# Eight taps, a moved mean product, an unspread plan, an earlier window sum and two rerouted transfers in a two-block model

## The chip, the cores and the metric

The kernel runs on one core of a Trainium2 chip. The metric is the device time of one execution in microseconds (us), median of three runs. The engines are PE (matrix products), DVE (vector), ACT (scalar), POOL (GpSimd) and SP, which here only issues transfers.

## What is computed

Two blocks of two layers each, width 1024, 512 tokens (the second block has 256 context tokens more, 768 in all), all in float32. The parts that the change touches:

```python
def _multiscale_pool(z, pool_w, pool_scale):      # first block, layer 0
    pooled = jnp.stack([_centred_mean_minus_self(zf[:, :, g], w) for g, w in enumerate((2, 4, 8, 16))], axis=2)
    y = jnp.einsum('bsgc,gcd->bsgd', pooled, pool_w)
    return y.reshape(nb, s, B_WIDTH) * pool_scale

def _conformer_conv(h, w_in, dw, dw_b, ln_g, ln_b, w_out):   # first block, layer 1
    a, g = jnp.split(h @ w_in, 2, axis=-1)
    z = a * jax.nn.sigmoid(g)
    z = _depthwise_conv(z, dw, dw_b)               # 31 taps per channel
    z = jax.nn.silu(_layer_norm(z, ln_g, ln_b))
    return z @ w_out

# second block, each layer
h_lat = h_lat + ml[2] * rms_norm(o_lat, g_post_mix[i])
f_lat = sqrelu_mlp(modulate(h_lat, g_pre_ff[i], ml[3], ml[4]), w_ff1[i], w_ff2[i])
h_lat = h_lat + ml[5] * rms_norm(f_lat, g_post_ff[i])
```

## The kernel before

The program is a row of stages. Each is a block in which every engine has its own instruction list, ordered by semaphores, and a barrier of all engines ends it. The weight stream alone runs across barriers. SP loads 1 MB weight blocks into a ring of four (line 219), in the order of use, and waits before each load until the block that had the slot is used. ACT casts a piece of a block to a high part (lines 247, 248, 283), DVE subtracts to make the low part (lines 262, 263, 294, called the split here), and PE computes three products per pair. Two pieces are in flight, so ACT can cast a piece only when PE has used the piece before last, and PE needs DVE's split before it begins a piece.

Side work rides on the stream. The modulation matrices ("ada") come as side blocks between the weight blocks. DVE adds up a side block over the eight row groups in place (lines 315 and 317, eight steps for one vector, which sum_side splits in two halves of four), and PE finishes with four tiny products (line 429). When a host matrix is in SPREAD, the halves that wait are taken by turns, about one half after each piece. Otherwise all that wait are taken after the last piece of a block. PE's side products follow the piece at which the second half was taken, and they free the side block's slot in the ring. "up0" has 22 blocks of two pieces and hosts 24 side blocks. In the same stage DVE adds two of three taps of a short convolution (lines 1124, 1126) after ACT has written the centre tap (line 1103), and multiplies by the gelu on every second piece (line 1131).

The mixer of the first layer computes v by token, then z in four feature pieces, then the token mixing (line 1203), then u in four pieces. DVE normalises v (lines 1297 to 1299) between the splits. POOL makes the window sums of z (lines 1241, 1246, 1247), 18 instructions in four groups; the last operations of group g wait for product g-2 of PE (line 1208).

The conformer stage computes a gated z in eight channel tiles. The 31 taps of a tile are divided: the first PE_TAPS[j] are products with diagonal matrices on PE (line 1381; ACT makes the diagonals, line 1414), and DVE adds the others (lines 1436, 1438) to two running sums and joins them (line 1442). PE goes on to the column means by products with ones (line 1392). The next stage takes the mean (line 1483), subtracts it, squares on ACT, sums the squares on PE (line 1478), and so on.

In the second block the residual of 768 tokens (3 MB) is parked in device memory while its place is used for other data. It is brought back by a transfer: in the stage "out0" the 1 MB of the context, in "ff2_0" all 3 MB. Both are output stages: PE computes the product in two halves of 512 columns, and for the second half DVE works tile by tile (lines 1632 to 1637). Ahead of its first tile it waits for the transfer (`dve.wait_ge(brought, 16)`, line 1629). POOL issues the transfer after it has fetched the gate rows. In ff2_0 it first waits for the split that frees the borrowed place:

```python
def bring_back(pool, first, pieces, brought):
    pool.wait_ge(weights.lo_made, first + pieces // 2 + n_borrowed // 2)
    nc.gpsimd.dma_start(flat_of(resid), parked).then_inc(brought, 16)
```

`weights.load(sp, name)` issues all loads up to four blocks beyond the stage's own; the last of them waits for the stage's last split.

Of the kernel before, what the change touches and what calls it, by code (L numbers as in the profile page):

```python
# [23 lines left out]
ALU = mybir.AluOpType  # L24
# [7 lines left out]
D = 1024  # L32
DK = D // P
# [14 lines left out]
FFN = ((8 * D // 3 + 127) // 128) * 128  # L48
FK = FFN // P
CONV_W = 31  # L50
PE_TAPS = [8] * 6 + [11, 26]
DFF = 4 * D
HD = 64
GRID_W = 64
# [55 lines left out]
}  # L110


SPREAD = ["up0", "up1", "ab_v"]
THIRD_SLOT = ["ab_out", "down0", "cv_out"]


# [243 lines left out]
def build(nc, dram, out_dram, debug=None):  # L360
# [783 lines left out]
    def sgu_pool_mixer(hT, out_stage):  # L1144
# [4 lines left out]
        with stage():  # L1149
            mixT = sb("mixT", [P, DK, SEQ])  # L1150
            left = LeftOperand("ab_out", lambda k: mixT[:, k:k + 2, :], SEQ)
            with stage():
# [26 lines left out]
                with nc.Block() as block:  # L1179
# [46 lines left out]
                    @block.gpsimd  # L1226
                    def _(pool):
                        step = Chain(pool, pool_step)
                        nc.gpsimd.memset(z[:, :, 0:PAD], 0.0).then_inc(zeroed, 1)
                        nc.gpsimd.memset(z[:, :, PAD + SEQ:ZW], 0.0).then_inc(zeroed, 1)  # L1230
                        pool.wait_ge(loaded, 16 * n_loads)
                        pool.wait_ge(zeroed, 2)
                        pool.wait_ge(normed, LAT_T)
                        for g in range(4):
                            window = 2 << g
                            src = z[:, g, :]
                            pool.wait_ge(evac, Z0 + g + 1)
                            for level in range(g + 1):
                                lo, off = (2 << level) - 1, 1 << level
                                dst = sums[:, level % 2, :]  # L1240
                                step(nc.gpsimd.tensor_tensor(dst[:, lo:ZW], src[:, lo:ZW], src[:, lo - off:ZW - off], ALU.add))
                                src = dst
                            at = PAD + window // 2 - 1
                            if g >= 2:
                                pool.wait_ge(pool_mm, g - 1)
                            step(nc.gpsimd.tensor_tensor(pooled[:, g % 2, :], src[:, at:at + SEQ], inv_count[:, g, :], ALU.mult))
                            nc.gpsimd.tensor_tensor(pooled[:, g % 2, :], pooled[:, g % 2, :], z[:, g, PAD:PAD + SEQ], ALU.subtract).then_inc(pooled_made, 1)
                            pool.wait_ge(pooled_made, g + 1)
# [93 lines left out]

    def conformer_mixer(hT, affine, out_stage):
        HALF = CONV_W // 2
        MEAN_BANK = 0
        with stage():
            zc = sb("conv_out", [P, DK, SEQ])
            left = LeftOperand("cv_out", lambda k: zc[:, k:k + 2, :], SEQ)
            with stage():
# [10 lines left out]
                with nc.Block() as block:  # L1360
# [11 lines left out]
                    @block.tensor  # L1372
                    def _(pe):
                        def tap_products(j):

                            pe.wait_ge(diag_made, j + 1)
                            pe.wait_ge(evac, 2 * (j + 1))
                            if j >= 1:
                                pe.wait_ge(started, j)
                            for i in range(PE_TAPS[j]):  # L1380
                                last = nc.tensor.matmul(ps[SIDE_BANK][:], diag[:, j % 2, i, :], zp[:, j, i:i + SEQ],
                                                        start=(i == 0), stop=(i == PE_TAPS[j] - 1))
                            last.then_inc(taps_mm, 1)

                        def after_piece(piece):
                            if piece % 2 and piece > 1:
                                tap_products(piece // 2 - 1)
                        feature_products(pe, "cv_in", hT, [slice(0, SEQ)], evac, after_piece=after_piece)
                        tap_products(DK - 1)
                        for j in range(DK):  # L1390
                            pe.wait_ge(chained, j + 1)
                            nc.tensor.matmul(ps[MEAN_BANK][:], ones[:], zc[:, j, :], start=(j == 0), stop=(j == DK - 1))

                    @block.scalar
                    def _(act):
# [66 lines left out]
            with stage():  # L1462
                cols = sb("cv_ln_columns", [P, 2, DK])
                sq = sb("squares", [P, 2, SEQ])
                mean, inv = sb("mean", [P, SEQ]), sb("inv_std", [P, SEQ])
                loaded, centred, squared = sem("loaded"), sem("centred"), sem("squared")
                chained, var_ready, root_ready, normed, applied = sem("vector_step"), sem("var_ready"), sem("root_ready"), sem("normed"), sem("silu_done")
                sq_used = sem("square_used")
                with nc.Block() as block:
# [4 lines left out]
                    @block.tensor  # L1474
                    def _(pe):
                        for j in range(DK):
                            pe.wait_ge(squared, j + 1)
                            nc.tensor.matmul(ps[1][:], ones[:], sq[:, j % 2, :], start=(j == 0), stop=(j == DK - 1)).then_inc(sq_used, 1)

                    @block.vector  # L1480
                    def _(dve):
                        step = Chain(dve, chained)
                        step(nc.vector.tensor_scalar(mean[:], ps[MEAN_BANK][:], 1.0 / D, None, ALU.mult))
                        for j in range(DK):
                            nc.vector.tensor_tensor(zc[:, j, :], zc[:, j, :], mean[:], ALU.subtract).then_inc(centred, 1)
                        dve.wait_ge(sq_used, DK)
                        nc.vector.tensor_scalar(inv[:], ps[1][:], 1.0 / D, LN_EPS, ALU.mult, ALU.add).then_inc(var_ready, 1)
                        dve.wait_ge(root_ready, 1)
                        step(nc.vector.reciprocal(inv[:], inv[:]))
                        dve.wait_ge(centred, DK)  # L1490
                        for j in range(DK):
                            nc.vector.tensor_tensor(zc[:, j, :], zc[:, j, :], inv[:], ALU.mult).then_inc(normed, 1)
                        weights.lo_early(dve, "cv_out", left.share(0))
# [39 lines left out]
    def out_product_rms_stage(name, left, tiles, gates, bring_back=None, store=False):  # L1533
# [4 lines left out]
        with stage():  # L1538
# [13 lines left out]
            with nc.Block() as block:  # L1552
                @block.gpsimd
                def _(pool):
                    gate_rows_by_dma(pool, gates, spilled, gate_landed)
                    if bring_back is not None:
                        bring_back(pool, first, pieces, brought)

                @block.sync
                def _(sp):  # L1560
                    weights.load(sp, name)
                    if store:
                        for i, t in enumerate(tiles):
                            sp.wait_ge(added, i + 1)
# [79 lines left out]
    def ffn2_stages(layer, tiles):  # L1644
# [4 lines left out]
        with stage():  # L1649
# [8 lines left out]
            with stage():  # L1658
# [8 lines left out]
                with stage():  # L1667
# [3 lines left out]
                    with nc.Block() as block:  # L1671
# [23 lines left out]
                        def _(dve):  # L1695
# [7 lines left out]
                            if left.ahead:  # L1703
                                weights.lo_early(dve, down, left.share(0))
                            side_sums(dve, up)
            def bring_back(pool, first, pieces, brought):
                pool.wait_ge(weights.lo_made, first + pieces // 2 + n_borrowed // 2)
                nc.gpsimd.dma_start(flat_of(resid), parked).then_inc(brought, 16)
            out_product_rms_stage(down, left, tiles, gates2(layer, FF_GATE, 2 if n_borrowed else 1),
                                  bring_back if n_borrowed else None, store=layer == DEPTH - 1)  # L1710

# [1326 lines left out]
    def second_block():  # L3038
        for layer in range(DEPTH):
            tiles = all_tiles if layer == 0 else lat_tiles  # L3040
            streams = 2 if layer == 0 else 1
            with stage():
                bring = None
                if layer == 0:
# [3 lines left out]
                    left = LeftOperand("out0", lambda k: mixT[:, k:k + 2, :], TOK, ahead=False)  # L3048
                    dump("rwkv", mixT[:, 0:4, :])

                    def bring(pool, first, pieces, brought):
                        nc.gpsimd.dma_start(flat_of(resid)[:, 0:CTX_T * D], parked[:, 0:CTX_T * D]).then_inc(brought, 16)
                else:
                    mixT, left = odd_mixer()
                    dump("odd", mixT[:])
# [216 lines left out]
```

## Time and profile before

| what | value |
|---|---|
| median of three runs | 3683.64 us (3683.22 to 3686.53) |
| the profiled execution | 3686.53 us, span 3684.6 us |
| mean granted PE clock | 0.941 |
| busy: PE, DVE, ACT, POOL | 3230.6, 2201.8, 1289.6, 139.9 us |
| weight and data traffic | 342.67 MB, mean 93 GB/s |

The span runs from the first to the last instruction of one profiled execution; all positions below are us from its start. The line numbers are those of the kernel before.

### The profile page before, as it was taken

The numbers are of one execution on the slowest core, as the hardware profiler recorded it, in microseconds if no ns is written. First come the engines' busy times: TensorE is split into PE (matmuls) and PEld (weight loads), VectorE is DVE, ScalarE is ACT, GpSimd is POOL, SyncE is SP. The second block draws the span as 40 slices with busy tenths as digits, with TensorE's granted clock in tenths as the row PEclk, the third lists the DMA queues.
The fourth block names the chain that finished last, engine by engine and source line by source line (L and its number), as shares of the span: only waits on it lengthen the run. The fifth ranks groups of instructions, "written<-read, shape, count | busy, mean of one in ns | idle before, by whom it ended". The sixth has DMA issues, their size and how long they took to land. (4 is left out here: it accounts for less than half of the span.)

```text
span 3684.6 us, 62774 instructions
## 1 busy us (share of the span) xinstructions
PE 3230.6 (88%) x26414; PEld 2617.1 (71%) x26414; DVE 2201.8 (60%) x3942; ACT 1289.6 (35%) x2191; POOL 139.9 (4%) x180
## 2 busy tenths in 40 slices
PE   6989998988999958976776777999998999879999
PEld 5767876646887757844765766887887777658787
DVE  7678866785786466766445445554334556663344
ACT  2333334334333332154324325222234225642243
POOL 0200001000000001000101100000000000000000
PEclk8989999998999979988988998999999999989999
DMA  7524462202335212310000022322221242022231
GB/s 291 166 105 182 183 182 88 69 12 78 135 137 138 99 48 105 125 53 30 5 32 12 5 72 82 113 103 98 75 92 58 103 138 70 1 97 92 82 96 69
DMA packets 64424, 342.67 MB, mean 93 GB/s; under 512 B 15120, under 2 KB 16656, under 8 KB 28432
## 3 DMA queue, kind: packets, MB, share of 16 engines
q1 hardware_dynamic: 61616, 326.82, 26.1%
q0 software_dynamic: 2528, 11.84, 0.9%
q8 instruction: 209, 3.42, 0.4%
q14 instruction: 71, 0.58, 0.1%
HBM read 327.84 MB, written 10.79 MB: 92 GB/s over the span
## 5 line engine op out<-in xcount | busy, mean ns | idle before, releaser
L263 DVE TENSOR_TENSOR weight_lo<-weight_ring,weight_hi 128x1024 fp32r<-128x1024 f32 x341 | 423.0, 1242 | 152.5 <-ACT weight_hi L248 147.6
L248 ACT CAST weight_hi<-weight_ring 128x1024 fp32r<-128x1024 f32 x341 | 355.9, 1044 | 177.4 <-PE banks L420 91.9
L418 PE MATMUL banks<-hT_hi.1,weight_hi 128*128 128x512 f32 x896 | 365.9, 408 | 24.8 <-PEq L381 22.7
L419 PE MATMUL banks<-hT_lo.1,weight_hi 128*128 128x512 f32 x896 | 358.8, 400 | 0.0
L420 PE MATMUL banks<-hT_hi.1,weight_lo 128*128 128x512 f32 x896 | 358.5, 400 | 0.0
L418 PEld LDWEIGHTS banks<-hT_hi.1,weight_hi 128*128 128x128 f32 x896 | 171.4, 191 | 68.2 <-issue 25.7
L419 PEld LDWEIGHTS banks<-hT_lo.1,weight_hi 128*128 128x128 f32 x896 | 171.3, 191 | 41.5 <-issue 1.9
L420 PEld LDWEIGHTS banks<-hT_hi.1,weight_lo 128*128 128x128 f32 x896 | 171.0, 191 | 41.9
L418 PE MATMUL banks<-hT_hi.3,weight_hi 128*128 128x512 f32 (+1 forms) x512 | 175.5, 343 | 7.9 <-PEq L381 7.9
L419 PE MATMUL banks<-hT_lo.3,weight_hi 128*128 128x512 f32 (+1 forms) x512 | 174.3, 341 | 0.0
L420 PE MATMUL banks<-hT_hi.3,weight_lo 128*128 128x512 f32 (+1 forms) x512 | 174.3, 340 | 0.0
L317 DVE SCALAR_TENSOR_TENSOR side_sum<-weight_ring,silu_c2.1,side_sum 128x256 f32<-128x256 f32 x336 | 160.3, 477 | 0.0
L317 DVE SCALAR_TENSOR_TENSOR weight_ring<-weight_ring,silu_c2.1 128x256 f32<-128x256 f32 x336 | 160.2, 477 | 0.0
L517 PE MATMUL banks<-weight_hi,left_hi.6 128*128 128x512 f32 x360 | 144.5, 401 | 8.3 <-DVE weight_lo L263 8.3
L520 PE MATMUL banks<-weight_lo,left_hi.6 128*128 128x512 f32 x360 | 142.5, 396 | 0.0
L519 PE MATMUL banks<-weight_hi,left_lo.6 128*128 128x512 f32 x360 | 141.9, 394 | 0.0
L317 DVE SCALAR_TENSOR_TENSOR weight_ring<-weight_ring,silu_c1.1 128x256 f32<-128x256 f32 x280 | 135.6, 484 | 10.5
L418 PE MATMUL banks<-hT_hi.2,weight_hi 128*128 128x256 f32 (+1 forms) x352 | 123.6, 351 | 17.1 <-PEq L381 17.1
L420 PE MATMUL banks<-hT_hi.2,weight_lo 128*128 128x256 f32 (+1 forms) x352 | 122.0, 347 | 0.0
L419 PE MATMUL banks<-hT_lo.2,weight_hi 128*128 128x256 f32 (+1 forms) x352 | 122.0, 346 | 0.0
L262 DVE TENSOR_TENSOR left_lo.6<-ff_hidden.1,left_hi.6 128x1536 fp32r<-128x1536 f32 x24 | 42.2, 1760 | 130.9 <-ACT weight_hi L248 130.9
L2666 ACT COPY residual.1<-banks 128x512 f32<-128x512 f32 x120 | 70.3, 586 | 140.6 <-PE banks L2824 139.4
(744 smaller groups left out, 7759.1 us busy)
## 6 DMA issues: line engine op xcount, KB each, us to landing
weight_ring<-ff SPq DMA_DIRECT2D x64, 1024.0 KB, 4.9
weight_ring<-ada SPq DMA_DIRECT2D x48, 1024.0 KB, 5.0
weight_ring<-up SPq DMA_DIRECT2D x44, 1024.0 KB, 6.9
weight_ring<-ada_ffn SPq DMA_DIRECT2D x24, 1024.0 KB, 5.0
weight_ring<-down SPq DMA_DIRECT2D x20, 1024.0 KB, 4.9
weight_ring<-ada_mix SPq DMA_DIRECT2D x16, 1024.0 KB, 4.9
first_blocks.1<-ada_mix SPq DMA_DIRECT2D x8, 1024.0 KB, 11.8
weight_ring<-cv_in SPq DMA_DIRECT2D x8, 1024.0 KB, 5.0
```

The lines of the kernel that those rows point to most:

```text
L248: self.nc.scalar.copy(hi, raw).then_inc(self.hi_made, 1)
L262: self.nc.vector.tensor_tensor(x[2], x[0], x[1].bitcast(F32), ALU.subtract)
L263: self.nc.vector.tensor_tensor(lo, raw, hi.bitcast(F32), ALU.subtract).then_inc(self.lo_made, 1)
L317: ins = self.nc.vector.scalar_tensor_tensor(out=to, in0=w[:, k, :], scalar=vec[:, k, v:v + 1], in1=to, op0=ALU.mult, op1=ALU.add)
L418: nc.tensor.matmul(out, w_hi, x_hi, start=first, stop=False)
L419: nc.tensor.matmul(out, w_hi, x_lo, start=False, stop=False)
L420: return nc.tensor.matmul(out, w_lo, x_hi, start=False, stop=last)
L517: one = nc.tensor.matmul(out, xh, hi[:, kk, :], start=(k == 0), stop=False)
L519: nc.tensor.matmul(out, xl, hi[:, kk, :], start=False, stop=False)
L520: last = nc.tensor.matmul(out, xh, lo[:, kk, :], start=False, stop=(k == k_tiles - 1))
L2666: nc.scalar.copy(XT_flat[c % 2], pair(c, X_AT, 4 * CH)).then_inc(xt_copied[c % 2], 1)
```

## The change

Five edits in one. The last channel tile's taps on PE go from 26 to 18, so DVE gets 13 instead of 5. "up0" leaves SPREAD. POOL's window sums no longer wait for the normalised v. The eight mean products move from the end of the conformer stage to the start of the next, and DVE waits for them there. The two transfers that bring the residual back are issued by SP, behind the stage's weight loads, instead of by POOL.

```diff
-PE_TAPS = [8] * 6 + [11, 26]
+PE_TAPS = [8] * 6 + [11, 18]
-SPREAD = ["up0", "up1", "ab_v"]
+SPREAD = ["up1", "ab_v"]
                         pool.wait_ge(zeroed, 2)
-                        pool.wait_ge(normed, LAT_T)
                         for g in range(4):
...
                         tap_products(DK - 1)
-                        for j in range(DK):
-                            pe.wait_ge(chained, j + 1)
-                            nc.tensor.matmul(ps[MEAN_BANK][:], ones[:], zc[:, j, :], start=(j == 0), stop=(j == DK - 1))
...
                     @block.tensor
                     def _(pe):
                         for j in range(DK):
+                            last = nc.tensor.matmul(ps[0][:], ones[:], zc[:, j, :], start=(j == 0), stop=(j == DK - 1))
+                        last.then_inc(mm_mean, 1)
+                        for j in range(DK):
                             pe.wait_ge(squared, j + 1)
...
-                        step(nc.vector.tensor_scalar(mean[:], ps[MEAN_BANK][:], 1.0 / D, None, ALU.mult))
+                        dve.wait_ge(mm_mean, 1)
+                        step(nc.vector.tensor_scalar(mean[:], ps[0][:], 1.0 / D, None, ALU.mult))
...
                     gate_rows_by_dma(pool, gates, spilled, gate_landed)
-                    if bring_back is not None:
-                        bring_back(pool, first, pieces, brought)
 
                 @block.sync
                 def _(sp):
                     weights.load(sp, name)
+                    if bring_back is not None:
+                        bring_back(sp, first, pieces, brought)
...
-            def bring_back(pool, first, pieces, brought):
-                pool.wait_ge(weights.lo_made, first + pieces // 2 + n_borrowed // 2)
-                nc.gpsimd.dma_start(flat_of(resid), parked).then_inc(brought, 16)
+            def bring_back(sp, first, pieces, brought):
+                sp.wait_ge(weights.lo_made, first + pieces // 2 + n_borrowed // 2)
+                sp.dma_start(flat_of(resid), parked).then_inc(brought, 16)
...
-                    def bring(pool, first, pieces, brought):
-                        nc.gpsimd.dma_start(flat_of(resid)[:, 0:CTX_T * D], parked[:, 0:CTX_T * D]).then_inc(brought, 16)
+                    def bring(sp, first, pieces, brought):
+                        sp.dma_start(flat_of(resid)[:, 0:CTX_T * D], parked[:, 0:CTX_T * D]).then_inc(brought, 16)
```

## Rows read from the trace of the kernel before

**Rows 1.** Busy us, share of the span, instructions, of each engine.

```profile
PE 3230.6 (88%) x26414; PEld 2617.1 (71%) x26414; DVE 2201.8 (60%) x3942; ACT 1289.6 (35%) x2191; POOL 139.9 (4%) x180
```

**Rows 2.** Windows, the stretch of up0; PEclk is the granted clock.

```profile
core 0: us, PE busy (x) PEld busy (x) DVE busy (x) ACT busy (x) POOL busy (x), PEclk, DMA share, GB/s
...
210.00:490.00 280.00, 264.93 (x1161) 214.88 (x1162) 233.95 (x370) 95.97 (x123) 0.91 (x1) 0.96 0.48 176
```

**Rows 3.** Timeline of POOL in the mixer: start, duration, then idle and releaser.

```profile
104.96 1.84 POOL L1241 TENSOR_TENSOR window_sums.1<-z_padded.1 128x543 f32<-128x543 f32 x1 [60.11 <-DVE v.1 L1299]
...
122.05 1.09 POOL L1246 TENSOR_TENSOR pooled.1<-window_sums.1,inv_count.1 128x512 f32<-128x512 f32 x1 [2.02 <-PE banks L1208]
```

**Rows 4.** Timeline of ACT and DVE in the mixer.

```profile
89.53 0.58 ACT L1254 COPY z_padded.1<-banks 128x512 f32<-128x512 f32 x1
...
104.03 0.69 DVE L1299 TENSOR_TENSOR v.1<-v.1,sgu_bias.1 128x512 f32<-128x512 f32 x1
```

**Rows 5.** Timeline of POOL and DVE where both work, a later stage.

```profile
1461.25 1.59 POOL L2265 TENSOR_TENSOR qk_b.1<-qk_b.1,mixT.2 128x512 f32<-128x512 f32 x1 [0.63 <-DVE qk_b.1 L2309]
...
1450.62 1.36 DVE L315 TENSOR_SCALAR side_sum<-weight_ring,silu_c2.1 128x256 f32<-128x256 f32 x1
1452.02 0.35 DVE L315 TENSOR_SCALAR weight_ring<-weight_ring,silu_c2.1 128x256 f32<-128x256 f32 x1
...
1461.73 1.40 DVE L2326 SCALAR_TENSOR_TENSOR r.1<-gate_rows.1,recurrence_columns.1,r.1 128x255 f32<-128x255 f32 x1
```

**Rows 6.** Timeline of PE, the token mixing of the mixer.

```profile
106.00 3.82 PE L1203 MATMUL banks<-ws_transposed.1,v.1 128*128 128x128 f32 x32
```

**Rows 7.** Windows at up0's end and after the conformer: PEclk.

```profile
480.00:486.00 6.00, 0.00 (x0) 0.00 (x0) 5.27 (x9) 1.04 (x2) 0.00 (x0) 0.66 0.91 344
486.00:492.00 6.00, 5.84 (x14) 4.61 (x15) 2.42 (x3) 2.00 (x2) 0.91 (x1) 0.50 0.81 181
...
830.00:832.00 2.00, 1.68 (x4) 1.42 (x5) 0.06 (x1) 1.65 (x2) 0.95 (x1) 0.50 0.33 78
```

**Rows 8.** Timeline of DVE and ACT in up0: a normal, then the doubled block.

```profile
330.85 0.75 DVE L1124 SCALAR_TENSOR_TENSOR ffn_conv.1<-banks,ffn_taps.1,ffn_conv.1 128x511 f32<-128x511 f32 x1 [0.34 <-ACT ffn_conv.1 L1103]
...
332.30 1.22 DVE L263 TENSOR_TENSOR weight_lo<-weight_ring,weight_hi 128x1024 fp32r<-128x1024 f32 x1
...
336.10 0.78 ACT L1103 ACTIVATE ffn_conv.1<-banks,ffn_taps.1 128x512 f32<-128x512 f32 x1 [4.35 <-PE banks L420]
...
340.37 0.34 DVE L315 TENSOR_SCALAR weight_ring<-weight_ring,silu_c1.1 128x256 f32<-128x256 f32 x1
340.75 3.67 DVE L317 SCALAR_TENSOR_TENSOR weight_ring<-weight_ring,silu_c1.1 128x256 f32<-128x256 f32 x7
...
348.17 1.23 DVE L263 TENSOR_TENSOR weight_lo<-weight_ring,weight_hi 128x1024 fp32r<-128x1024 f32 x1 [2.31 <-ACT weight_hi L248]
```

**Rows 9.** Timeline of PE and DVE at the conformer's end.

```profile
797.42 7.03 PE L1392 MATMUL banks<-conv_out.1,ones.1 128*128 128x512 f32 x16
...
799.22 0.75 DVE L1438 SCALAR_TENSOR_TENSOR second_sum.1<-glu_padded.1,conv_taps.1,second_sum.1 128x512 f32<-128x512 f32 x1
...
800.55 0.75 DVE L1438 SCALAR_TENSOR_TENSOR second_sum.1<-glu_padded.1,conv_taps.1,second_sum.1 128x512 f32<-128x512 f32 x1
...
805.21 0.69 DVE L1483 TENSOR_SCALAR mean.1<-banks 128x512 f32<-128x512 f32 x1 [3.19 <-PEq L381]
```

**Rows 10.** Timeline of the queues of SP and POOL in out0 and ff2_0.

```profile
2239.82 0.33 SPq L219 DMA_DIRECT2D weight_ring<-ff  x1
...
2829.93 0.33 SPq L219 DMA_DIRECT2D weight_ring<-ada  x1
...
2729.40 0.53 POOL L1708 DMA_DIRECT2D residual.1<-parked_residual  x1 [150.63 <-DVE weight_lo L263]
```

**Rows 11.** DMA issues: count, KB each, median us from issue to landing.

```profile
weight_ring<-ada SPq DMA_DIRECT2D x48, 1024.0 KB, 5.0
...
parked_residual<-residual.1 SPq DMA_DIRECT2D x2, 3072.0 KB, 9.7
...
residual.1<-parked_residual POOLq DMA_DIRECT2D x1, 3072.0 KB, 12.0
```

**Rows 12.** Timeline of DVE, first tile of out0's and ff2_0's second half.

```profile
2242.39 0.16 DVE L1632 TENSOR_TENSOR inv_rms.1<-sums_of_squares.1 128x1 f32<-128x1 f32 x1 [1.40 <-ACT product.1 L1594]
...
2832.52 0.16 DVE L1632 TENSOR_TENSOR inv_rms.2<-sums_of_squares.2 128x1 f32<-128x1 f32 x1 [2.61 <-ACT product.2 L1594]
```

More of the change, by code:

```diff
@@ L1344, in conformer_mixer @@
         HALF = CONV_W // 2
-        MEAN_BANK = 0
         with stage():
@@ L1465, in conformer_mixer @@
                 mean, inv = sb("mean", [P, SEQ]), sb("inv_std", [P, SEQ])
-                loaded, centred, squared = sem("loaded"), sem("centred"), sem("squared")
+                loaded, mm_mean, centred, squared, mm_var = sem("loaded"), sem("mean_product"), sem("centred"), sem("squared"), sem("var_product")
                 chained, var_ready, root_ready, normed, applied = sem("vector_step"), sem("var_ready"), sem("root_ready"), sem("normed"), sem("silu_done")
```

## The prediction

> **What bounds the kernel now.** I read the totals first. PE is busy 88% of the span, DVE 60%, ACT 35%, POOL 4% [rows 1], so nearly everywhere the time is PE's, and an edit costs what it makes PE wait. Next came the stretch of "up0" among the windows: PE is busy for 265 of its 280 us and DVE for 234 [rows 2]. Last came the order of work inside each edited stretch (the timeline of one engine at a time), which shows how late the instruction that releases PE may be. Stages end in a barrier of all engines, and nothing runs across one but weight loads. A late stage therefore passes its whole delay on, and delays of different stages add.
>
> **Part 1: window sums freed from the norm.** POOL now begins at 104.96, right after DVE's last norm step (104.03 + 0.69 = 104.72) [rows 3, 4]. Without that wait it needs only the first z column, which ACT has copied by 90.1 (89.53 + 0.58) [rows 4]. Ten POOL instructions (3 for the first window, 4 for the second, 3 sums of the third) move from 105 to 120 us into 90 to 113 us. Everything behind them stays, because the multiply at 122.05 waits for PE's first pooled product [rows 3]; POOL's early finish buys PE nothing. The place they move to is where DVE is full: norm steps, splits and side sums nearly back to back until 104.72.
>
> What does DVE pay? A scalar_tensor_tensor of 255 elements, whose like comes every 0.51 us in a row of seven [rows 8], takes 1.40 us beside a POOL instruction that began at 1461.25 and ends at 1462.84; a tensor_scalar takes 1.36 us beside POOL and 0.35 us right after [rows 5]. The two exclude each other, instruction by instruction, at 0.9 to 1.0 us for each POOL instruction met. Nine of the ten meet DVE work (the first falls in DVE's wait for the root): 9 x 0.92 = 8.3 us later. The slack is small: the norm ends at 104.72 and PE's token mixing, which waits for it, starts at 106.00 [rows 4, 6]. So 8.3 - 1.3 = 7.0 us on PE. A split between the norm steps is late as well and stops PE earlier; that stall lies inside the 7.0. PE then idles some 5 us. At up0's end an idle PE was granted 0.66 of full speed and then 0.50 (the 1.2 GHz level) for 6 us of work [rows 7]; I add 1.0 for a part of that. **Part 1: +8** (bounds: five meetings and no clock loss, +3.3; ten at 1.01 and 2.5 for the clock, +11.3).
>
> The Trainium skill's page "SBUF — State Buffer" (Who interferes with whom) says that a DVE instruction contends with a GpSimd one that reads SBUF if it has two SBUF inputs or is in a two-port mode, and that the later one blocks fully. Read narrowly, by the first half alone, a norm step with one input would pass freely, and the term would lose some 1 us. The blocked tensor_scalar above has one SBUF tensor input, so the row bears out the second half, and I count all.
>
> **Part 2: up0 without the spread.** Each of 22 blocks (two pieces A, B) is followed by a side block, two of them by two: 24. A side block is 8 DVE steps (0.38 + 7 x 0.51 = 3.95 us). Now four follow the split of B and four that of the next A; afterwards all eight follow that of B. In a normal block the next A split, which ends at 333.52, is put off by 1.65 us to 335.17 (the eight end 2.0 later than the four, and DVE had 0.34 us of wait before 330.85) [rows 8]. PE wants it when B ends, about 335.9, as ACT reads B's bank at 336.10 [rows 8]. 0.6 us are left: no cost in about 20 blocks.
> At the doubled block 16 steps come in a row. From 340.37 they end at 348.3, two conv steps and the next split at 351.0. PE has finished B and its side products at 348.4, so it waits 2.6 us. Today it waits there too, some 1.6 us: the split comes at 348.17 because ACT's cast, and before it the weight load, is late [rows 8]. That load will start about 6 us sooner, since side blocks are freed one piece earlier. Net **+1** (bounds: -1.6, nothing left of today's wait; +8, 0.4 us in each of 20 blocks).
>
> **Part 3: the conformer's tail.** PE's last work today is 26 taps of 0.88 us each (two passes of 0.44), then 8 mean products of the same kind: 16 passes in 7.03 us, until 804.45; DVE takes the mean at 805.21, after the barrier (0.76), having been done 3.19 us before, at 802.02 [rows 9]. After the change PE does 18 taps and is free at 797.42 - 8 x 0.88 = 790.4. DVE's last convolution still starts where it did, behind the one before it, and has 13 taps instead of 5: 8 x 0.665 (half of 800.55 - 799.22 [rows 9]) = 5.3 us more, 802.02 + 5.3 = 807.3, barrier at 808.1. Of the 7.0 us taken off PE nothing arrives, for DVE has become the end of the stage. ACT's 8 fewer diagonals were hidden.
> Then the eight mean products, until now beside DVE's taps for all but 2.4 us, stand alone at the next stage's start: 16 passes, 7.0 us. PE comes to them after 17 us of idleness. After the 15 us one before 830.3 it was granted 0.50 from 830 to 832 [rows 7]. I take 3 us at half, 1.5 lost, and 0.3 for the first weight load. 808.1 + 7.0 + 1.5 + 0.3 = 816.9 against 805.21: **+12** (bounds: full clock +10; 6 us at half, as at up0's end, +13.5). By parts: 4 for the taps alone, 8 for the moved products.
>
> **Part 4: the residual brought back by SP.** The two transfers move from POOL's queue to behind SP's weight loads. Those run four blocks ahead, so the last one waits for the stage's last split: SP issues it at 2239.82 (out0) and 2829.93 (ff2_0) [rows 10]. Today POOL issues ff2_0's at 2729.40 [rows 10], 100 us ahead, and out0's right after the gate rows. Each ring wait of SP now holds the transfer too, and it then shares the DMA engines with the 1 MB load just ahead of it.
> In ff2_0: 3 MB plus 1 MB. The same 3 MB landed 12.0 us after POOL's issue, the 3 MB parked by SP 9.7 after its own, a lone load takes 5.0 [rows 11]. From 2830.3 I take 11.6, near POOL's: 2841.9. DVE waits for it before its first tile, which starts at 2832.52 today [rows 12]: +9.4 (bounds 9.7 and 14: +7.5 and +12). In out0: 1 MB plus 1 MB, 5.0 for one and 2.2 more for the second: 2239.8 + 7.2 = 2247.0 against 2242.39 [rows 12]: +4.6 (5.0 alone from 2240.2: +2.8; two of 5.0 in series: +7.4). DVE then works its six tiles one after another as before, ACT following it, and nothing later in the stage has slack. **Part 4: +14**. POOL's queue gains nothing; it carried nothing else that was waited for.
>
> The Trainium skill, same page (SBUF: two separate sides), says that POOL-issued transfers starve while DVE works in two-port mode and advises SP. If the 12.0 us contain such a wait, the transfer from SP lands sooner than I take, 9.7 giving +7.5; but it was issued 100 us ahead of its use, so there was no waiting to save.
>
> **The sum.** 8 + 1 + 12 + 14 = +35. The profiled execution took 3686.5 (span 3684.6), 2.9 above the median of 3683.64, so 3721.5 for its like and **3719** for a median.
>
> **Rivals.** (a) The shared port matters little: DVE meets four or five POOL instructions, part 1 is +3, total +30, 3714. For: the third window's sums may come when DVE is past its norm. Against: DVE is full there. (b) DVE becomes the bound of up0: each block's A split slips past PE's 0.6 us, 20 x 0.4 = 8 on top of 35: 3727. For: DVE is busy 234 of 280 us and gets 4 us bursts. Against: its waits stand behind the burst. (c) The clock: PE's new gaps leave it at half for 6 us in part 1, part 3 and once more after ff2_0, +6: 3725. (d) Not slower: the clock the other way. PE's mean grant is 0.94, up0's stretch has 0.96 [rows 2]; should the new gaps keep it at full level where it is now at half, 1 us returns for each 2 us of matmul, and 70 us of such stretches would be needed to meet 35; at 100 us it is 3669. For: nothing in the rows; up0 holds only some 20 of them. (e) Part 4 misses: the transfers land before DVE's last split, 14 less, 3705. Against: SP's queue cannot pass its load at 2829.93.
>
> **How the numbers follow.** Main case 0.60, (a) 0.13, (b) 0.09, (c) 0.10, (d) 0.02, (e) 0.06. The main case's own range adds neighbouring bounds, not all at one end: 3709 to 3729. Reaching to (a) to (c) and near (e): 3704 to 3732. About 0.2% (7 us) is what this measurement tells from no change; slower by more 0.96, within 0.02, faster 0.02.
>
> **What would show it.** Part 1: POOL's first sum near 91, DVE's 0.69 us steps at 1.3 to 1.6, mixing near 113. Part 2: eight sum steps in a row without a PE wait, one wait of 2 to 3 us. Part 3: DVE's final add at 807 on this scale, the mean products in the next stage, the first at half clock, 12 us from old to new mean. Part 4: DVE waits for a DMA at both places, 4 to 5 and 9 to 10 us. Wrong would be: no lengthened DVE steps, or a residual transfer that has landed when DVE asks.

## The result: 1.2% slower, and the profile after

The changed kernel took 3727.22 us (median of 4 executions, 3724.63 to 3731.65) and the kernel before, beside it on the same chip, 3684.35 (3683.22 to 3686.53): +42.9 us, ratio 1.0119, 95% interval 1.0106 to 1.0132. The forecast was 3719 with a range of 3704 to 3732. The profiled execution took 3725.03, with a span of 3722.9 against 3684.6 (+38.3) and a mean granted clock of 0.937 against 0.941. Positions below are us from the span's start; behind line 1232 the changed kernel's line numbers are one to five lower than those of the kernel before.

First the totals, from the page:

```profile
PE 3230.0 (87%) x26398; PEld 2617.4 (70%) x26398; DVE 2212.8 (59%) x3950; ACT 1287.0 (35%) x2183; POOL 138.8 (4%) x178
```

PE is as busy as in [rows 1], in a span 38 us longer: it waits more. To see where, take from PE's timeline the first product of each stage that follows a barrier:

```profile
145.34 0.47 PE L517 MATMUL banks<-weight_hi,left_ahead_hi.1 128*128 128x512 f32 x1 [1.52 <-PEq L381]
224.73 0.76 PE L418 MATMUL banks<-hT_hi.1,weight_hi 128*128 128x512 f32 x1 [7.94 <-PEq L381]
495.91 0.77 PE L517 MATMUL banks<-weight_hi,left_ahead_hi.2 128*128 128x512 f32 x1 [6.29 <-PEq L381]
640.16 0.77 PE L418 MATMUL banks<-hT_hi.1,weight_hi 128*128 128x512 f32 x1 [8.27 <-PEq L381]
854.26 0.76 PE L517 MATMUL banks<-weight_hi,left_ahead_hi.3 128*128 128x512 f32 x1 [15.27 <-PEq L381]
```

In the kernel before the same five products start at 137.23, 216.86, 486.16, 631.60 and 830.32. The lag grows to 8.1 over the mixer, to 9.8 over up0, falls to 8.6 over down0, and stands at 23.9 after the conformer. Then it stays at 24.1 to 24.5 as far as 1910, dips to 21.0 at 2156, in stages that no edit touches, and ends at 38.3 behind out0 and ff2_0. The loss lies in the edited places.

**The mixer.** Timelines of POOL, DVE and PE:

```profile
88.92 2.02 POOL L1240 TENSOR_TENSOR window_sums.1<-z_padded.1 128x543 f32<-128x543 f32 x1 [43.98 <-ACT z_padded.1 L1253]
91.01 1.37 POOL L1245 TENSOR_TENSOR pooled.1<-window_sums.1,inv_count.1 128x512 f32<-128x512 f32 x1
...
130.16 1.09 POOL L1245 TENSOR_TENSOR pooled.1<-window_sums.1,inv_count.1 128x512 f32<-128x512 f32 x1 [25.56 <-PE banks L1208]
```

```profile
90.50 0.72 DVE L1296 TENSOR_SCALAR v.1<-v.1,mean_var.1,inv_std.1 128x512 f32<-128x512 f32 x1
91.25 1.68 DVE L1297 TENSOR_TENSOR v.1<-v.1,sgu_gain.1 128x512 f32<-128x512 f32 x1
...
98.98 2.29 DVE L263 TENSOR_TENSOR weight_lo<-weight_ring,weight_hi 128x1024 fp32r<-128x1024 f32 x1
101.19 1.18 DVE L315 TENSOR_SCALAR weight_ring<-weight_ring,silu_c1.1 128x256 f32<-128x256 f32 x1
102.41 5.15 DVE L317 SCALAR_TENSOR_TENSOR weight_ring<-weight_ring,silu_c1.1 128x256 f32<-128x256 f32 x7
...
110.69 0.69 DVE L1298 TENSOR_TENSOR v.1<-v.1,sgu_bias.1 128x512 f32<-128x512 f32 x1
```

```profile
101.32 0.50 PE L418 MATMUL banks<-hT_hi.1,weight_hi 128*128 128x512 f32 x1 [2.52 <-DVE weight_lo L263]
...
111.52 6.40 PE L1203 MATMUL banks<-ws_transposed.1,v.1 128*128 128x128 f32 x32 [3.31 <-DVE v.1 L1298]
```

While POOL works (until 104.6), DVE's steps take 1.2 to 1.7 us (the first of them 0.72) and a split 2.29 instead of 1.22; behind the side sums they are back at 0.69 [rows 4]. PE now waits for DVE twice, and the token mixing takes 6.40 instead of 3.82 us [rows 6]. The windows show why: the granted clock, the third number from the end, was 0.50 over its first part, where the kernel before had 1.00.

```profile
111.00:114.00 3.00, 2.48 (x11) 2.51 (x12) 3.00 (x4) 0.00 (x0) 0.00 (x0) 0.50 0.47 194
```

At 130.16 POOL waits 25.6 us for PE: its head start bought nothing.

**Up0.** PE's only wait over 0.5 us between its first and last product:

```profile
358.51 0.50 PE L418 MATMUL banks<-hT_hi.1,weight_hi 128*128 128x512 f32 x1 [1.97 <-DVE weight_lo L263]
```

It stands behind 16 side steps in a row, the doubled block, where the kernel before waited 1.37 us. Behind the single blocks of eight steps PE does not wait. But the clock fell behind this wait, and it did not in the kernel before (1.00 from 349.5 to 352):

```profile
358.50:360.00 1.50, 1.49 (x5) 1.25 (x6) 1.37 (x2) 0.43 (x1) 0.00 (x0) 0.77 1.02 426
360.00:362.00 2.00, 2.00 (x6) 1.51 (x6) 1.99 (x3) 0.00 (x0) 0.00 (x0) 0.50 0.98 414
362.00:364.00 2.00, 2.00 (x9) 1.58 (x8) 1.79 (x5) 0.00 (x0) 0.00 (x0) 0.82 0.66 172
```

I estimate the loss from these rows at 1.5 x 0.23 + 2.0 x 0.50 + 2.0 x 0.18 = 1.7 us, more than the wait itself grew.

**The conformer's end.** DVE's last sum, PE's products, DVE's mean, and the granted clock over them:

```profile
816.05 0.69 DVE L1437 TENSOR_TENSOR conv_out.1<-conv_out.1,second_sum.1 128x512 f32<-128x512 f32 x1
827.64 0.69 DVE L1482 TENSOR_SCALAR mean.1<-banks 128x512 f32<-128x512 f32 x1 [10.90 <-PE banks L1472]
```

```profile
817.52 10.08 PE L1472 MATMUL banks<-conv_out.1,ones.1 128*128 128x512 f32 x16 [17.39 <-PEq L381]
829.78 9.21 PE L1476 MATMUL banks<-squares.1,ones.1 128*128 128x512 f32 x16 [2.17 <-ACT squares.1 L1500]
```

```profile
819.00:822.00 3.00, 3.00 (x5) 1.09 (x4) 0.00 (x0) 0.00 (x0) 0.00 (x0) 0.50 0.00 0
...
824.00:826.00 2.00, 2.00 (x6) 0.95 (x5) 0.00 (x0) 0.00 (x0) 0.00 (x0) 1.00 0.00 0
...
830.00:832.00 2.00, 2.00 (x4) 0.70 (x3) 2.00 (x5) 0.90 (x2) 0.00 (x0) 0.59 0.03 8
```

The mean products stand alone and take 10.08 us against 7.03 in [rows 9]. The clock was granted at 0.50, the 1.2 GHz level, until about 823, and near it again when the squares' products began after PE's next pause of 2.2 us; those took 9.21 us, 7.71 before. Whether that last loss belongs to the edit is taken up behind e5 and e6.

**Out0 and ff2_0.** SP's issues, and DVE's first tile:

```profile
2263.28 0.33 SPq L219 DMA_DIRECT2D weight_ring<-ff  x1
2263.66 0.43 SPq L3051 DMA_DIRECT2D residual.1<-parked_residual  x1
...
2857.89 0.33 SPq L219 DMA_DIRECT2D weight_ring<-ada  x1
2858.26 0.43 SPq L1707 DMA_DIRECT2D residual.1<-parked_residual  x1
```

```profile
2270.64 0.16 DVE L1631 TENSOR_TENSOR inv_rms.1<-sums_of_squares.1 128x1 f32<-128x1 f32 x1 [6.18 <-DMA residual.1<-parked_residual]
...
2870.65 0.16 DVE L1631 TENSOR_TENSOR inv_rms.2<-sums_of_squares.2 128x1 f32<-128x1 f32 x1 [12.78 <-DMA residual.1<-parked_residual]
```

The releaser is a DMA in both places. DVE idles 6.18 and 12.78 us where it idled 1.40 and 2.61 for ACT [rows 12]: 4.8 and 10.2 more.

### The profile page after: what moved, and what is told of

It reads as the page before. It is cut to its first block and busy times, and to the rows that moved or that the text cites. A ratio compares the mean times of both kernels' runs of the same rounds, so it can differ in the third digit from the quotient of the medians.

```text
span 3722.9 us, 62741 instructions
## 1 busy us (share of the span) xinstructions
PE 3230.0 (87%) x26398; PEld 2617.4 (70%) x26398; DVE 2212.8 (59%) x3950; ACT 1287.0 (35%) x2183; POOL 138.8 (4%) x178
```

## The experiments

Twelve kernels, each the kernel before with the edit named, in three groups of four; each group ran on a chip of its own with the kernel before beside it. That kernel's median was 3689.90 in the first group (21 executions, 3682.6 to 3694.2), 3687.60 in the second (27) and 3686.48 in the third (33, 3678.0 to 3694.9). Executions of one kernel thus spread by 12 to 17 us. I therefore give two numbers, the difference of the medians, and what the edited stage itself grew in the profiled execution, by the same stage starts as above. The second is the sharper one, but it is one execution each, and a stage that no edit touches can differ by 1 to 3 us between two profiles too.

### The parts one by one

**e1_pool**, window sums alone:

```diff
-                        pool.wait_ge(normed, LAT_T)
```

> The kernel before with the first edit alone: POOL's window sums no longer wait for the normalised v. Theory (POOL and DVE shut each other out, instruction by instruction, where DVE is full; then PE idles and restarts at half clock): +8 us over the kernel before, of which about 6.7 are DVE's delay of its last norm step and about 2.6 are the token mixing at the 1.2 GHz level (6.4 instead of 3.8 us), less the 1.3 of slack. Nothing after the mixer changes, so the whole run is +8. Rival (port matters little): +3. Rival (the delay is absorbed by the weight stream later, since the ring gets full while PE idles): under +4 in the whole run although the mixer is 8 longer.

Measured: 3699.99, +10.1 (ratio 1.0026, 1.0017 to 1.0035); the mixer +8.8. DVE's norm (first step to last) takes 20.9 us against 12.8; the mixing 6.45 us. As in the changed kernel. Both rivals are out: the lag is 11.1 us at 217 and 11.2 at 1574, so nothing is absorbed later. (Of these 11, 2.3 arose in the stage behind the mixer, which e2 and e3 show as well, without this edit.)

**e2_spread**:

```diff
-SPREAD = ["up0", "up1", "ab_v"]
+SPREAD = ["up1", "ab_v"]
```

> The kernel before with up0 taken out of SPREAD alone. Theory (eight side steps in a row cost nothing behind a normal block's split, and 1 us at the one doubled block): +1 to +2 us, from the stage of up0 alone, with perhaps some tenths given back in down0 (whose first loads came earlier), so the run is +0.5 to +2. Rival (DVE becomes the bound of up0, 0.4 us in each of 20 blocks): +8. Rival (the stage ends earlier since slots of the ring are freed earlier): -1.5.

Measured: 3691.25, +1.4 (1.0007, 0.9997 to 1.0016). Up0 +2.4, down0 -0.9, and the same wait of 1.97 us at the doubled block, with the same clock behind it: 0.80, 0.50 and 0.90 in 353.5 to 356, to 358 and to 360. DVE does not become up0's bound. The size of the first theory holds, but by terms that it did not have: the wait grew by 0.6 us, and the rest of the 2.4 is mainly this clock (1.7 us, estimated as above).

**e3_tail**: both conformer edits of the diff, nothing else.

> The kernel before with the conformer's edits alone: 18 taps instead of 26 for the last tile on PE, and the eight mean products moved to the next stage. Theory (DVE's 13 taps end the stage, then the mean products stand alone, at half clock since PE has idled 17 us, and the squares' products after them too): +14 to +15.5 us in this kernel as in the one with all edits, of which 4 are taps, 10 the mean products, 1.5 the squares' products. Rival (part of the 15 came from the other edits' disturbance, such as the clock or the ring's state): +12, as it was first estimated with only 3 us at half clock.

Measured: 3704.15, +14.3 (1.0034, 1.0021 to 1.0047); the stages from the conformer's start to cv_out's +14.0, with mean products of 9.49 us and squares' products of 9.37 us. The interval of the whole run, +8 to +17 us, holds the rival's +12 too; the stages speak for the theory, and the loss is the conformer's own.

**e4_sp**: the bring-back by SP, as in the diff.

> The kernel before with the bring-back by SP alone: the two transfers of the residual are issued by SP behind the stage's weight loads. Theory (they come late, since SP's queue holds them behind a load that waits for the stage's last split; DVE waits for the landing, and nothing after it has slack): +15 us, 5 in out0 and 10 in ff2_0. Rival (a wait of 5 and one of 10 are partly made good by weight loads that run ahead across the barrier): under +11.

Measured: 3704.28, +14.4 (1.0034, 1.0019 to 1.0048). DVE waits 6.26 and 12.44 us for the DMA. Nothing is made good later: the lag behind ff2_0, 16.7 us against the profile of before, is 16.8 at the end. The four parts alone add up to 10.1 + 1.35 + 14.25 + 14.4 = 40.1 of the 42.9 us: within the spread nothing points to an interaction.

### Where the bring-back stands in SP's queue

**e7_sp_early**: SP issues both transfers, but in out0 ahead of the stage's loads, and in ff2_0 amid them (`load` gets a limit `upto` for this, not shown):

```diff
+                    if bring_back is not None:
+                        middle = weights.pieces[first + pieces // 2 + 4][0] + RING + 1
+                        weights.load(sp, name, upto=middle if pieces > 16 else weights.loads)
+                        bring_back(sp, first, pieces, brought)
                     weights.load(sp, name)
```

> The residual brought back by SP as in the changed kernel, but not behind the stage's last weight load: in out0 ahead of the stage's loads, in ff2_0 amid them, as soon as the borrowed place is free (the load ahead of it waits for the same split). Theory (the cost of 15 us is the place in SP's queue, not that SP issues it): 0 within 2 us of the kernel before, DVE waits for no DMA at either place. Rival (SP's transfer of 3 MB stands ahead of weight loads in the same queue and delays them, so that PE waits in mid-stream): +2 to +10 in the stage of ff2_0. Rival (SP's transfers are slower in themselves): DVE waits in out0, +3.

Measured: 3686.54, -1.1 (1.0000, 0.9991 to 1.0010). SP issues at 2174.46 and 2745.95, and DVE waits for ACT again:

```profile
2241.90 0.16 DVE L1636 TENSOR_TENSOR inv_rms.1<-sums_of_squares.1 128x1 f32<-128x1 f32 x1 [1.41 <-ACT product.1 L1598]
...
2832.17 0.16 DVE L1636 TENSOR_TENSOR inv_rms.2<-sums_of_squares.2 128x1 f32<-128x1 f32 x1 [2.61 <-ACT product.2 L1598]
```

Between 2562 and 2840 PE is busy for 270.1 us, 269.7 in the kernel before, so the weight loads behind the 3 MB lose nothing either. The whole cost of part 4 is the place behind the last load, not the queue that issues.

### The conformer's tail taken apart

**e5_taps**:

```diff
-PE_TAPS = [8] * 6 + [11, 26]
+PE_TAPS = [8] * 6 + [11, 18]
```

> The kernel before with 18 instead of 26 taps for the last tile on PE, and nothing else; the mean products stay where they are and follow DVE's sums one by one. Theory (DVE's last convolution ends the stage, eight steps of 0.665 later; PE's last mean product waits for it): the mean is taken at 809 to 810 on the scale of the kernel before, +4 to +5, and PE, whose mean products wait for DVE, has idled enough for a part of them to run at half clock, which costs nothing as all but the last lie beside DVE. The run is +4 to +5. Rival (the half clock after PE's idle time is at its work here as well, 1.7 us or more on the last product and the squares' products): +6 to +7.

**e6_mean**: the mean products moved, 26 taps kept.

> The kernel before with the eight mean products moved to the next stage, and nothing else: PE keeps its 26 taps. PE is free at 797.4, DVE at 802.0, so PE idles 5.4 us instead of 17. Theory (the products cost 7.0 us alone and the half clock costs 3 more only after the long idle time): the mean at 802.8 + 7.0 + 0.3 = 810.1, +5, and after it no loss in the squares; the run +5. If the idle time of 5.4 us is enough for half clock: +8 at the mean, +9.5 in the run. Rival (taps and mean products add plainly, 4 and 11): +11.

Measured: e5 3696.93, +9.3 (1.0023, 1.0013 to 1.0033), its stages +8.0; e6 3695.83, +8.2 (1.0017, 1.0007 to 1.0026), its stages +6.1. Both miss. The taps alone cost about twice what was expected; the rival of e5 had the mechanism, but priced it at 6 to 7. These are the rows of PE's timeline in e5:

```profile
808.20 2.07 PE L1392 MATMUL banks<-conv_out.1,ones.1 128*128 128x512 f32 x2 [8.07 <-DVE conv_out.1 L1442]
813.17 9.98 PE L1478 MATMUL banks<-squares.1,ones.1 128*128 128x512 f32 x16 [2.90 <-ACT squares.1 L1501]
```

The last mean product alone comes after 8.07 us of waiting and takes 2.07 us, where the one before it took 1.12, and the squares' products 9.98 instead of 7.71; the clock stood at 0.50 from 808.2 to 816, through the pause between them. By stage starts, 5.8 of the 8.0 us had come by the mean and 2.3 came at the squares. In e6 the pause before the mean products was 5.20 us, and they took 8.67, between 7.03 and 10.08, while the squares' stayed at 7.71.

The squares' products need a caution. In seven of the nine profiles whose conformer is not edited (the kernel before, e1, e4, e7, e9, e10, e11) they took 7.70 or 7.71 us. In the other two, e2 and e12 below, they were slow behind the same pause:

```profile
812.33 9.40 PE L1478 MATMUL banks<-squares.1,ones.1 128*128 128x512 f32 x16 [2.89 <-ACT squares.1 L1501]
...
805.79 9.26 PE L1482 MATMUL banks<-squares.1,ones.1 128*128 128x512 f32 x16 [2.89 <-ACT squares.1 L1507]
```

So this half clock also comes without any edit to the conformer, in some executions. All four profiles with 18 taps on PE have it (9.21 to 9.98), which points to the taps, but how much of these 1.5 to 2.3 us is the edit's is not shown.

**e8_warm**: the tail of e3, and work for PE in the pause:

```diff
                         tap_products(DK - 1)
+                        pe.wait_ge(chained, 1)
+                        for _ in range(17):
+                            nc.tensor.matmul(ps[0][:], ones[:], zc[:, 0, :], start=True, stop=True)
```

> The conformer's edits as in the run of the tail alone (+14.3), and in PE's idle time of 17 us at the stage's end 17 products of 0.88 us into a bank that nobody reads (they add nothing to the output). Theory (3 us of the mean products and 1.5 of the squares are the half clock after that idle time): the granted clock stays at 1, the mean products take 7.0 instead of 10.1 us, the squares' phase 7.7 instead of 9.2, and the run is 4 to 4.5 below the tail alone, +10 over the kernel before. Rival (the 10.1 us are the products' own time when nothing runs beside them, reads of zc or the barrier): no change, +14.3.

Measured: 3700.82, +13.2 (1.0032, 1.0020 to 1.0044); the stages +13.0, 1.0 less than e3. The filler ran until 803.4, the barrier still made PE pause, and the clock fell behind that pause:

```profile
806.18 8.80 PE L1476 MATMUL banks<-conv_out.1,ones.1 128*128 128x512 f32 x16 [2.77 <-PEq L381]
817.15 9.21 PE L1480 MATMUL banks<-squares.1,ones.1 128*128 128x512 f32 x16 [2.17 <-ACT squares.1 L1504]
```

```profile
803.00:806.00 3.00, 0.40 (x1) 0.00 (x0) 2.36 (x4) 0.00 (x0) 0.00 (x0) 1.00 0.00 0
...
808.00:811.00 3.00, 3.00 (x5) 1.05 (x4) 0.00 (x0) 0.00 (x0) 0.00 (x0) 0.53 0.00 0
811.00:815.00 4.00, 3.98 (x10) 1.48 (x8) 0.00 (x0) 0.00 (x0) 0.00 (x0) 1.00 0.00 0
```

The rival (10 us is their own time) is refuted: at 0.53 three us hold five of the passes, at full clock four us hold ten. But the theory's size is refuted too: of 4.5 us the filler saved 1.0, and the squares' products gained almost nothing. At full clock behind the filler PE paused 2.77 us and the clock fell; it did not fall behind the 2.90 us ahead of the squares' products in the kernel before. The length of the pause alone does not decide.

### POOL's window sums by dose

**e9_three** and **e10_seven** put POOL's wait behind the first (`if g == 1`) and the second group (`if g == 2`), so 3 and 7 POOL instructions run beside the norm:

```diff
-                        pool.wait_ge(normed, LAT_T)
                         for g in range(4):
+                            if g == 1:
+                                pool.wait_ge(normed, LAT_T)
```

> The kernel before, with POOL's wait for the normalised v put behind the first of the four window groups: 3 POOL instructions instead of 10 run beside DVE's norm. Theory (each POOL instruction met costs DVE 0.9 to 1.0, and 1.28 us of slack lie before the token mixing): two or three met, 1.8 to 2.7 us later on DVE, so the mixing starts 0.5 to 1.4 later than before and at full clock; the mixer +0.5 to +1.5, the run within 0.2% of no change. Rival (an early POOL start costs as a whole, not by instructions met): +8 as with all ten.

> The same with POOL's wait behind the second group: 7 POOL instructions run beside DVE's norm. Theory: with all ten the norm's end came 6.7 later; seven of them give 4.5 to 6, of which 1.28 are slack, and the mixing starts 3.2 to 4.7 later; PE's wait before it is then 1 to 2.5 us, so it may keep the full clock. The mixer +3.5 to +7 (the upper end if the mixing runs at half clock). Rival (as a whole): +8.

**e11_warmmix**: all ten early, and a filler ahead of PE's wait for the norm:

```diff
+                        for _ in range(12):
+                            nc.tensor.matmul(ps[MIX0 % NROT][:, 0:P], ones[:], ones[:], start=True, stop=True)
                         pe.wait_ge(normed, LAT_T)
```

> The first edit alone (all ten POOL instructions early, +8.8 in the mixer's stage), and 12 products of ones by ones (128 columns) put ahead of PE's wait for the norm, into a bank that the token mixing then overwrites. They fill 3 us of PE's 3.3 us pause. Theory (2.6 us of the 8.0 are the token mixing at the 1.2 GHz level after PE's two pauses): the mixing takes 3.8 instead of 6.4 us and the stage is +5.5 to +6.2. Rival (the level falls by the pause of 2.5 us before it, which stays, or by what comes with the change on DVE): the mixing stays at 6.4 and the stage at +8.8.

PE's token mixing in e9, e10 and e11:

```profile
106.96 3.81 PE L1203 MATMUL banks<-ws_transposed.1,v.1 128*128 128x128 f32 x32 [0.69 <-DVE v.1 L1300]
```

```profile
109.86 6.65 PE L1203 MATMUL banks<-ws_transposed.1,v.1 128*128 128x128 f32 x32 [2.71 <-DVE v.1 L1300]
```

```profile
108.98 2.92 PE L1199 MATMUL banks<-ones.1 128*128 128x128 f32 x24
112.33 3.84 PE L1205 MATMUL banks<-ws_transposed.1,v.1 128*128 128x128 f32 x32 [0.42 <-DVE v.1 L1300]
```

| early POOL instructions | DVE's norm, us (before 12.8) | mixing, us | mixer | whole run |
|---|---|---|---|---|
| 3 (e9) | 14.8 | 3.81 | +0.9 | 3688.56, +2.1 (0.9993 to 1.0015) |
| 7 (e10) | 18.4 | 6.65 | +6.7 | 3692.07, +5.6 (1.0001 to 1.0019) |
| 10 (e1) | 20.9 | 6.45 | +8.8 | +10.1 |
| 10 and filler (e11) | 20.6 | 3.84 | +6.4 | 3694.22, +7.7 (1.0008 to 1.0028) |

The cost follows the dose: 2.0, 5.6 and 8.0 us of norm. The windows give the clock of the mixing: 0.50 from 110 to 113 in e10, 1.00 in e9 and e11. So the half clock is a cost of its own: filling PE's pause gives the mixing its 3.8 us back and takes 2.4 off the stage. Here 0.42 us lie between filler and work, and the filler did what it could not do in e8, where the barrier left 2.77.

### A version to beat both

**e12_keepwarm**: none of the edits, but fillers in pauses that the kernel before has: 13 products behind the squares' products, and at the end of each of the three stages that turn the normalised residual:

```diff
+                    pe.wait_ge(mod_act, HALF_F)
+                    pe.wait_ge(mod_dve, DK - HALF_F)
+                    for _ in range(3):
+                        nc.tensor.matmul(ps[2][:], ones[:], resid[:, tiles[0], 0:BANK], start=True, stop=True)
...
+                        for _ in range(13):
+                            nc.tensor.matmul(ps[2][:], ones[:], sq[:, 0, :], start=True, stop=True)
```

> The kernel before with none of the edits, and products that nobody reads in pauses of PE which it already has: 13 of 0.88 us in the 15.3 us behind the squares' products of the conformer, and 3 at the end of each of the three stages that turn the normalised residual (7.4 to 7.8 us of pause). The stages after these pauses begin at the 1.2 GHz level today and stay there for 3 to 6 us. Theory (the level follows what PE did just before, so work in the pause gives it back): 1 to 2 us less after the conformer and 1 to 3 us less at each of the three, -4 to -8 us, faster than both kernels. Rival (a pause of 2 to 3 us at the barrier is enough for the lower level, as in the run with the filled tail): 0 within 2 us.

Measured: 3686.51, +0.0 (0.9996, 0.9987 to 1.0005). The mean granted clock rose from 0.941 to 0.946, but not where it was wanted. Windows across the conformer's end:

```profile
814.00:826.00 12.00, 12.00 (x29) 5.16 (x28) 8.95 (x10) 7.16 (x9) 0.00 (x0) 1.00 0.00 0
826.00:830.00 4.00, 0.21 (x1) 0.00 (x0) 2.36 (x2) 3.57 (x6) 0.00 (x0) 0.93 0.00 0
830.00:836.00 6.00, 5.67 (x13) 4.46 (x14) 2.42 (x3) 1.99 (x2) 0.95 (x1) 0.50 0.71 177
```

Twelve us at full clock, a pause of 4 us at the barrier, and six us of real work at 0.50. The full clock was given to products that nobody reads. Behind the three stages with the other fillers the pauses were 3.98, 3.51 and 4.48 us, and the first 3 us of work were granted 0.74, 0.50 and 0.52, against 0.50 each before. This profile also has the slow squares' products (9.26 us). The rival holds. None of the kernels tried is shown to be faster than the kernel before.

## Why the prediction was right, and what it mis-sized

| | predicted | in the profiled execution | median of the part alone |
|---|---|---|---|
| 1, window sums | +8 | +8.1 | +10.1 |
| 2, up0 (with down0) | +1 | +1.9 - 1.2 = +0.7 | +1.4 |
| 3, conformer's tail | +12 | +15.4 | +14.3 |
| 4, bring-back | +14 | +4.8 + 10.2 = +15.0 | +14.4 |
| sum | +35 | 39.2, span +38.3 | 40.1, all together +42.9 |

**Part 1** came out at its number with its own terms a little off. DVE's norm stretched by 20.88 - 12.84 = 8.0 (forecast 8.3, nine meetings at 0.92), and the slack of 1.3 was there; but in the changed kernel's profile the norm also began 1.4 us sooner (90.50 against 91.88), so PE's mixing was 5.5 late instead of 7.0. The clock cost 2.6, not 1.0. These two misses cancel, and that is luck. In e1, where the norm began 0.8 sooner, the stage is +8.8. e9 to e11 show the mechanism and both terms. Rival (a), four or five meetings, is out: seven single steps are longer by 0.8 to 1.1 us each, and the seven side steps of line 317 by 1.5 together. The Trainium skill's page "SBUF — State Buffer" (Who interferes with whom) agrees in the reading that I took: a norm step with one SBUF tensor input, free by the narrow reading, took 1.46 us in e1 beside POOL and 0.55 otherwise. Who begins first matters as well: in e10 the same step began at 95.13, took 0.54 us, and POOL's sum of 95.26 took 1.35 instead of 1.09.

**Part 2** is right in its waits: none behind single blocks, one at the doubled block, 1.97 instead of 1.37, so 0.6 of the forecast 1.0. Its number is luck: the clock behind that wait, which it did not have, cost some 1.7 us more, and down0 came out 0.9 to 1.2 shorter in both profiles. I did not look for the cause of the latter; the profiles of e5 and e12, where up0 is not edited, have down0 1.4 us shorter too, so it need not come from the edit. Rival (b), +8 in up0, is out: e2's up0 grew by 2.4.

**Part 3** had the mechanism and the order of events: DVE's last sum ended at 816.74, 176.6 after the stage's start against 170.4 before, +6.2 (forecast 5.3, which e3 has); the barrier 0.8; then the products alone. Mis-sized is the step "I take 3 us at half, 1.5 lost". The products stood at half clock until about 823, some 6 us, and lost 3.0. The 0.3 for the first weight load did not show: the products began 0.8 after DVE's last sum, the barrier alone. To the mean that makes 13.9 instead of 11.7. And the prediction stopped at the mean, though the squares' products took 1.5 more, part of which may come without the edit (e2, e12). Rival (c), half clock for 6 us, came true in part 1 and here, but not behind ff2_0, where the first 3.3 us were at half before as well (0.50 then, 0.57 now); its 3725 is nearer to what was measured than the main case's 3719. The split "4 for the taps alone, 8 for the moved products" is wrong: alone they cost 8.0 and 6.1 (e5, e6). Each brings a pause and a half clock of its own; and that the taps' extra DVE time ends the stage was counted, but not that the last mean product then starts at half clock, and the squares' products perhaps by the same cause.

**Part 4** is right: issue behind the last load, landing 12.4 us after the issue (forecast 11.6), nothing later absorbs it, and e7 shows that the place in the queue is all of it. Rival (e) is out. The rule on transfers issued by POOL of the Trainium skill's page "SBUF — State Buffer" (SBUF: two separate sides), weighed in the prediction, showed no effect on the 3 MB: they landed 12.0 us after POOL's issue, 12.4 after SP's, and 13.2 in e7. The 1 MB of out0 landed 8.1 us after POOL's issue, beside a weight load issued 2.8 us before it, against 7.0 and 5.9 (e7) after SP's; which of the two made the difference, no run separates.

**The rest.** Of the 8 us between 3719 and 3727, 3.3 are these terms (38.3 - 35). The remaining 5 come from setting one execution against medians: the profiled execution of before was 2.2 above the median of its four, that of the changed kernel 2.2 below its own. Stage starts show where single executions differ: from 1574 to 1910, stages that no edit touches, the kernel before took 335.8 us and e6 343.1, of which 3.8 were given back by 2278, and 1 to 3 us at the stage behind the mixer. What sets that, I did not test, beyond the squares' products above (1.5 to 1.7 us in two of nine). Rival (d), the clock the other way, is out.

## What to carry to other kernels

Before a wait is taken away, see whether anybody waits for the work that it frees: POOL's sums came 15 us earlier and then waited 25.6 us for PE, while each of its instructions that met DVE cost almost a microsecond there. Put a transfer ahead of a queue's stalls rather than behind them, and price by the place in the queue, not by who issues. Where a change opens a pause in front of PE's work, add the half clock of the products behind it, and follow the chain past the first point measured; a filler helped where 0.42 us lay between it and the work, and hardly or not at all where a barrier left 2.77 and 4.12. And read the same untouched instructions in several profiles before a loss of 1 or 2 us is put down to an edit.

## What the runs showed of the hardware

- The granted clock fell behind shorter pauses than I had taken for needed: after 1.97 us (up0's doubled block, 0.50 soon after), 2.71 us (e10, mixing 6.65 instead of 3.82) and 2.77 us (e8, mean products 8.80 instead of 7.03), while the 0.69 us of e9 and 0.42 us of e11 left the mixing at 3.8.
- The length of the pause alone does not decide. The clock held at 1.00 behind 2.52 us in the changed kernel's mixer (101 to 104). Behind the 2.9 us ahead of the squares' products it held in seven profiles with the same instructions before it and fell in two.
- POOL suffers from a meeting as well: its first sum took 2.02 us in the changed kernel (beside a split of 1.22), and the same form took 1.09 at 133.57.
- Executions of one kernel spread more than the first four showed: 3678.0 to 3694.9 for the kernel before in 33 executions of the third group.
